# Attention in the second block: two heads to a step, in halves of TensorE's array

## What is computed

```python
logit_own = (jnp.einsum('hqd,hkd->hqk', qc, k_own).astype(jnp.float32) * scale
             - slopes[:, None, None] * dist_own)
logit_own = jnp.where(dist_own >= 0, logit_own, NEG_INF)
...
p = jax.nn.softmax(jnp.concatenate([logit_sel, logit_own], axis=-1), axis=-1).astype(v.dtype)
...
return (jnp.einsum('hqnk,hqnkd->hqd', p_sel, v_g)
        + jnp.einsum('hqk,hkd->hqd', p_own, v_own))
```

## Time and profile before

| | us |
|---|---|
| median of 3 runs | 2004.51 |
| lowest, highest | 2000.12, 2005.65 |
| the profiled execution | 2004.92 |
| its span in the trace | 2003.2 |
| TensorE busy | 1860.3 |
| VectorE busy | 1625.4 |
| ScalarE busy | 709.1 |
| GpSimd busy | 1053.3 |

### The profile page before, as it was taken

One profiled execution on the slowest core, in us unless ns is written; L12 is line 12 of the kernel. 1 busy time (PEld: TensorE's weight loads), 2 busy tenths in 40 slices (PEclk: granted clock), 3 DMA queues, 4 the chain that ended last, 5 costly groups with the idle time before them and its releaser, 6 DMA issues.

```text
span 2003.2 us, 27280 instructions
## 1 busy us (share of the span) xinstructions
PE 1860.3 (93%) x9487; PEld 1596.0 (80%) x9487; DVE 1625.4 (81%) x2566; ACT 709.1 (35%) x1097; POOL 1053.3 (53%) x654
## 2 busy tenths in 40 slices
PE   3997779999999999999999999999999989899985
PEld 2775557999999999999888887878886767778764
DVE  6979977978888888888499999999997867656656
ACT  2343133333333444444333333333334233233441
POOL 1332225588878655555577676767665533342001
PEclk8999789999999999999999999999999999999988
DMA  8241342489989788899899999999982222100011
GB/s 341 87 158 64 130 146 81 162 310 311 315 290 317 247 296 312 297 308 313 321 361 358 350 363 344 363 340 365 353 314 81 93 65 64 63 1 1 1 53 53
DMA packets 160805, 440.34 MB, mean 220 GB/s; under 512 B 13648, under 2 KB 63952, under 8 KB 157648
## 3 DMA queue, kind: packets, MB, share of 16 engines
q1 hardware_dynamic: 65296, 254.71, 36.5%
q0 software_dynamic: 36864, 134.23, 17.7%
q10 hardware_dynamic: 58560, 50.34, 7.6%
HBM read 386.80 MB, written 52.43 MB: 219 GB/s over the span
## 4 chain that ended last, share of the span: by engine, by line
PE 70%; DVE 17%; issue 4%; POOL 4%; ACT 2%; DMA 2%; SPq 0%; DVEq 0%; ACTq 0%; POOLq 0%; PEldq 0%
PE PS L908 30%; PE PS L1075 24%; PE PS L1038 4%; PE PS L1101 4%; POOL w_lo L801 3%; DVE arena L1668 2%; DVE arena L1627 2%; DVE arena L1834 1%; PE PS L1247 1%; PE PS L1229 1%; ACT w_hi L1269 1%; PE PS L923 1%; POOL arena L849 1%; PE PS L999 1%; DMA arena<-in_expert_u_rows,arena 1%
## 5 line engine op out<-in xcount | busy, mean ns | idle before, releaser
L801 POOL TENSOR_TENSOR w_lo<-raw,w_hi 128x1024 fp32r<-128x1024 f32 x300 | 725.0, 2417 | 763.1 <-ACT w_hi L1269 761.9
L1269 ACT ACTIVATE w_hi<-raw 128x1024 fp32r<-128x1024 f32 x332 | 351.9, 1060 | 976.4 <-PE PS L908 616.9
L908 PE MATMUL PS<-act_hi,w_hi 128*128 128x384 f32 (+1 forms) x1632 | 603.5, 370 | 42.3 <-DVE act_lo L1640 14.2
L908 PE MATMUL PS<-act_lo,w_hi 128*128 128x384 f32 (+1 forms) x1632 | 588.3, 360 | 0.0
L908 PE MATMUL PS<-act_hi,w_lo 128*128 128x384 f32 (+1 forms) x1632 | 588.1, 360 | 0.0
L908 PEld LDWEIGHTS PS<-act_hi,w_hi 128*128 128x128 f32 x1632 | 312.7, 192 | 96.4 <-issue 25.9
L908 PEld LDWEIGHTS PS<-act_lo,w_hi 128*128 128x128 f32 x1632 | 312.0, 191 | 25.9
L908 PEld LDWEIGHTS PS<-act_hi,w_lo 128*128 128x128 f32 x1632 | 312.9, 192 | 24.6 <-issue 1.4
L1075 PE MATMUL PS<-w_hi,act_hi 128*128 128x512 f32 x768 | 300.8, 392 | 5.2 <-ACT arena L1390 2.6
L1075 PE MATMUL PS<-w_hi,act_lo 128*128 128x512 f32 x768 | 300.0, 391 | 0.0
L1075 PE MATMUL PS<-w_lo,act_hi 128*128 128x512 f32 x768 | 299.6, 390 | 0.0
(11 more groups left out here) (317 smaller groups left out, 2004.2 us busy)
## 6 DMA issues: line engine op xcount, KB each, us to landing
raw<-in_expert_u SPq DMA_DIRECT2D x128, 512.0 KB
raw<-in_expert_v SPq DMA_DIRECT2D x128, 512.0 KB
raw<-in_w_in SPq DMA_DIRECT2D x52, 512.0 KB
arena<-in_w_ada SPq DMA_DIRECT2D x24, 1024.0 KB, 7.1
gel_d<-arena ACTq DMA_DIRECT2D x64, 384.0 KB
gates_d<-arena ACTq DMA_DIRECT2D x12, 2048.0 KB
arena<-gates_d SPq DMA_DIRECT2D x32, 768.0 KB, 7.1
arena<-gel_d SPq DMA_DIRECT2D x32, 768.0 KB
```

Of the source, the lines that this page charges most:

```text
L801: pool.tensor_tensor(w_lo[:, k % SPLIT, :], raw[:, k % RAW, :], w_hi[:, k % SPLIT, :].bitcast(F32), ALU.subtract).then_inc(lo_split, 1)
L908: mm = pe.matmul(PS[:, bank, 0:n_tok], w[:, k % SPLIT, c * P:(c + 1) * P], x[:, c, 0:n_tok], start=(i == 0 and n == 0), stop=(i == KC - 1 ...
L1269: act.activation(w_hi[:, k % SPLIT, :], raw[:, k % RAW, :], ACT.Copy).then_inc(hi_split, 1)
```

## The change

The units are numbered anew: by pair of heads m, then query block qb, then head e, so that units 2j and 2j + 1 are the two heads of a pair on the same queries.

- Logits: at an even slot TensorE issues both units' matmuls behind each other (step `both_logits`), one from rows 0 to 63 into bank 6, one from rows 64 to 127 into bank 1 (`S_BANK`). Odd slots issue none. VectorE and ScalarE still take a unit a slot.
- Value products: at odd slots alone, for both units, with the head alternating inside the loop over key blocks, so that the output goes to partitions 0 to 63 and 64 to 127 by turns. `PT[e]` replaces `PT[n % 2]`, which is the same buffer.
- All pairs of heads now use bank 0 for value products, since bank 1 holds logits; from the second pair on the first of them waits for `om_ready` of the pair before.
- Projections 32 to 39 swap their two banks; 32 now waits for the last read of bank 1.

```diff
-        if i >= 4:
+        if i >= 4 and i % 2:
             steps.append(("pv", i - 4))
         if 3 <= i < MH * TB + 3:
             steps.append(("turn", i - 3))
         if i < MH * TB:
+            if i % 2 == 0:
+                steps.append(("both_logits", i))
             steps.append(("logits", i))
...
-            return n % 4 if n < 12 else n % 2
+            return n % 4 if n < 12 else n % 2 if n < 32 else (n + 1) % 2
...
+        S_BANK = (6, 1)
...
-                    if 32 <= n < 34:
-                        pe.wait_ge(om_ready, 3 + n - 32)
+                    if n == 32:
+                        pe.wait_ge(l_ready, MH * TB)
+                    elif n == 33:
+                        pe.wait_ge(om_ready, 4)
...
-                if kind == "logits":
-                    m, e, qb = n // 8, n // 4 % 2, n % 4
+                if kind == "both_logits":
+                    m, qb = n // 8, n // 2 % 4
                     if n:
                         pe.wait_ge(l_ready, n)
                     else:
                         pe.wait_ge(rms_ready, 20)
                         pe.wait_ge(p_dve, 20)
-                    s64 = slice(64 * e, 64 * e + 64)
-                    pe.matmul(PS[:, 6, 0:(qb + 1) * P], aq[s64, m, qb * P:(qb + 1) * P],
-                              ak[s64, m, 0:(qb + 1) * P], start=True, stop=True).then_inc(s_full, 1)
+                        pe.wait_ge(p_dve, 32)
+                    for e in range(2):
+                        s64 = slice(64 * e, 64 * e + 64)
+                        pe.matmul(PS[:, S_BANK[e], 0:(qb + 1) * P], aq[s64, m, qb * P:(qb + 1) * P],
+                                  ak[s64, m, 0:(qb + 1) * P], start=True, stop=True).then_inc(s_full, 1)
...
-                    if n % 8 == 0 and m >= 2:
-                        pe.wait_ge(om_ready, m - 1)
+                    if n % 8 == 1 and m:
+                        pe.wait_ge(om_ready, m)
                     pe.wait_ge(pt_ready, n + 1)
                     for kb in range(qb + 1):
-                        mm = pe.matmul(PS[64 * e:64 * e + 64, m % 2, qb * P:(qb + 1) * P],
-                                       avt[:, kb, P * m + 64 * e:P * m + 64 * e + 64], PT[n % 2][:, kb * P:(kb + 1) * P],
-                                       start=(kb == 0), stop=(kb == qb))
-                    mm.then_inc(pv_done, 1)
+                        for e in range(2):
+                            mm = pe.matmul(PS[64 * e:64 * e + 64, 0, qb * P:(qb + 1) * P],
+                                           avt[:, kb, P * m + 64 * e:P * m + 64 * e + 64], PT[e][:, kb * P:(kb + 1) * P],
+                                           start=(kb == 0), stop=(kb == qb))
+                    mm.then_inc(pv_done, 2)
```

More of the change, by code:

```diff
@@ L142, in second_block_steps @@
     steps.append(("gturn", 0))
-    while len([st for st in steps if st[0] == "pv"]) < MH * TB:
+    while len([st for st in steps if st[0] == "pv"]) < MH * TB // 2:
         attend()
@@ L1234, in _ @@
                         pe.wait_ge(pt_ready, n)
-                    for kb in range(n % 4 + 1):
+                    for kb in range(n // 2 % 4 + 1):
                         mm = pe.transpose(PS[:, 7, kb * P:(kb + 1) * P], L[:, n % 3, kb * P:(kb + 1) * P], ident[:, :])
@@ L1504, in _ @@
                     if n >= 32:
-                        act.activation(mx[:, n - 32, :], PS[:, n % 2, :], ACT.Copy).then_inc(mx_ready, 1)
+                        act.activation(mx[:, n - 32, :], PS[:, unit_bank(n), :], ACT.Copy).then_inc(mx_ready, 1)
                 if kind == "tanh":
@@ L1583, in _ @@
                     act.wait_ge(nm_ready, n + 1)
-                    w = (n % 4 + 1) * P
+                    w = (n // 2 % 4 + 1) * P
                     act.activation(L[:, n % 3, 0:w], L[:, n % 3, 0:w], ACT.Exp, bias=nmax[:, n:n + 1],
@@ L2265, in _ @@
                 if kind == "logits":
-                    m, e, qb = n // 8, n // 4 % 2, n % 4
+                    m, qb, e = n // 8, n // 2 % 4, n % 2
                     w = (qb + 1) * P
@@ L2289, in _ @@
                         dve.wait_ge(alo_ready, 32 + m)
-                    v.scalar_tensor_tensor(out=tmp[:, m % 2, :], in0=PS[:, m % 2, :], scalar=0.5, in1=az[:, m, :],
+                    v.scalar_tensor_tensor(out=tmp[:, m % 2, :], in0=PS[:, 0, :], scalar=0.5, in1=az[:, m, :],
                                            op0=ALU.mult, op1=ALU.mult).then_inc(tmp_ready, 1)
```

6 lines of the change are left out of this document (3 added, 3 removed).

## The result

| | before | changed |
|---|---|---|
| median of 4 runs each, us | 2003.2 | 1984.41 |
| lowest, highest | 2000.12, 2005.65 | 1983.03, 1987.07 |
| ratio, with its 95% interval | | 0.9906 [0.9893, 0.9918] |
| span of the profiled execution | 2003.2 | 1981.3 |

The changed kernel is faster by 18.8 us, 0.9%. It is within 1.2 us of the rival "both heads fully side by side", which had 12%. That closeness is in part luck: the rival's mechanism is what happened, but its sum is near because terms that were off by up to 3.3 us cancel (at the end of "Why the forecast was off").

What follows compares the result with a forecast made beforehand. TensorE's time was taken as the kernel's time, busy 82.95 of 83.00 us beside the delta rule. Terms 7.5 + 8.9 - 1.1 - 0.3 - 0.35 - 1.0 + 0.3 = 13.95 us off 2004.9 gave 1991 us; range 1985.0 to 2002.5.

Steps and rivals of the forecast that it cites:

- both heads fully side by side: Rival: all passes of both heads overlap in logits and value products, 14.5 us of overlap, 1985.6 us in all; chance 0.12.
- Two halves of the array at once: Logits and value pairs up to scan 2: in-order overlap of two heads' passes saves 8.9 us, between 0 and 14.5.
- The floor of weight loads: Logits pairs with one key block: four loads of 128 columns fill the pair, cutting its saving from 3.9 to 3.5 us.
- Fewer changes of shape: TensorE's slots up to scan 2: fewer switches between logits, value products and transposes save 7.5 us, whatever the halves do.
- the levels: Stretch from the first logits to scan 2's end, forecast to shrink from 138.4 us by about 15.
- that case: Rival of no overlap: one tile waits for the other, shape savings 7.5 - 0.8 up to scan 2; 2001.3 us, chance 0.15.
- What is given back: Savings of TensorE lost where other engines set the time: 1.1 and 0.3 us up to scan 2, more ahead of scan 3.
- Place (a): 1855.88 to 1866.85 us, where VectorE and ScalarE set the end: TensorE's savings there are mostly lost, -1.1 us.
- The second chain: Chain of other engines ending at 1878.94 us, with slot 22 in it, which gets shorter for nothing: -0.3 us.
- The wider scaling ahead of scan 3: Between scan 2 and scan 3: VectorE's logits 30 grow to 512 columns, its scaling of unit 29 to 384: -0.35 us.
- Scan 3 at half clock: TensorE idles about 3.5 us ahead of scan 3, whose eight matmuls may run at half clock: 0 to 1.9, taken as -1.0 us.
- The tail: After 1928.97 us, units one by one at half clock: 7.4 us with overlap against 7.71 before, +0.3; without overlap -2.2.

## Why the forecast was off

**The step that failed** is the one under "Two halves of the array at once": "If the passes are started in order [...] the second pass of one head can run beside the first pass of the other, while the two passes of one matmul stay behind one another. Then 2m passes of alternating matmuls take m + 1 pass times." The rows of before showed no two tiles of one shape in a row, and the text chose the middle of a range from 0 to 14.5 us "because of the two-pass form". The two-pass form does not matter: both tiles take the same pass at the same time, and 2m passes take m. The term was 8.9; by starts the overlap was 14.4 us (7.7 and 6.7), the upper bound of 14.5, and TensorE's busy time fell by 13.6 of it (7.6 and 6.0). The floor of weight loads was wrong too. It charged 0.4 us for four loads of 128 columns one after another in a pair with k = 1. Such a pair took 0.42 us, as one matmul did (0.41), and in the pair with k = 4 shown above the loads start at 1820.612, .618, .720 and .727, in pairs as well.

**The rule on weight loads.** In this case the two heads of a value product share all rows and differ in columns only, and loads and passes of both ran side by side (1.03 us for sixteen passes, 1.89 in one half). The Trainium skill, TensorE: Matmul & The Clock Gate, Part 3, says that a load overlaps running matmuls only if its row group differs. The measurement differs and decides: the column halves overlapped as fully as the row halves. Even within one half a load ran beside a matmul: in the logits pair the loads at 1820.720 and .727 belong to the second passes, which start at 1821.147 and .153, so each started while its own half's first pass (from 1820.613 and .620) was running. The same part's price for a packed group, one matmul's duration plus some 4 ns a tile, is borne out, with 7 ns here.

**Fewer changes of shape**: right in kind, too small by 1.5 us. 7.5 us was the sum; TensorE's time fell by 9.0 in the run with pairs and no overlap, 6.5 of them in the levels (6.7 was the forecast of that case). The constants from the earlier trace rows hold, and so does the one that no row showed: one transpose ahead of head groups takes 0.16 us (1809.44 to 1809.60), 0.11 of it the pass, so 0.05 was right. Two things are not in the sum. The stretch has two passes of value products and two transposes fewer than before (124 for 126, and 64 for 66), which is 0.4 us. And two transposes ahead of logits take 0.31 us (1820.30 to 1820.61), where they took 0.37 in the earlier trace rows; at 15 such places that is up to 0.9 us, an estimate. Why they became cheaper is open.

**What is given back**: right in kind, far too small, and it is one of the forecast's own signs of being wrong: VectorE's and ScalarE's steps ended TensorE's waits inside the levels. The levels lost 5.3 us to new idle time, where the forecast charged 1.4, and 2.0 with full overlap. Place (a) came out at its price: idle 1.4 before, 2.6 after, 1.2 more for 1.1 forecast. The second chain was put at 0.3 and cost 0.95. The other 3 us are at four places that the forecast did not name, 1869.27 and 1878.44 above all. It had looked for chains in the trace of before where they already ended TensorE's waits, and taken VectorE's share of 70% for room. What it should have done is to follow the pattern of `tokens` to all four chunks: in the kernel before ScalarE's copy of the transposes (line 1592) stood behind the same scaling (1544) at the third chunk, just hidden by TensorE's own work (in order of time, start us, us, instruction):

```profile
1884.95 1.14 ACT L1544 ACTIVATE arena<-PS,small 128x128 f32<-128x128 f32 x4 [2.43 <-DVEq L2220]
...
1886.35 0.28 ACT L1592 ACTIVATE arena<-PS 128x128 f32<-128x128 f32 x1 [0.27 <-ACT arena L1544]
```

Against full overlap, the levels were to be 22.0 - 2.0 = 20.0 us shorter and became 17.3 shorter.

**The wider scaling ahead of scan 3**: -0.35 forecast, -0.54 measured. From ScalarE's squares to scan 3 the chain grew from 7.79 to 8.12 us, the 0.35 to within rounding. The other 0.2 lie ahead of the squares (0.93 and 1.13 us behind the first matmul that follows scan 2), where ScalarE now finishes an exponential before it copies scan 2's result. **Scan 3 at half clock**: -1.0 forecast, -1.5 measured. The mechanism is shown: TensorE idled 3.77 us ahead of it, it ran at 0.50, and 6.51 us came back as soon as TensorE was kept busy, in both runs of the changed kernel kept busy.

**The tail**: +0.3 forecast, +2.7 measured, and it is the same mechanism with its sign turned. The forecast computed the tail at half clock as in the earlier trace rows. Now the idle time and the clock's fall come earlier, at scan 3, and the clock is back when the tail runs. That it is the clock and not the pairs is shown by the two kernels kept busy: 4.87 us for the old tail at full clock and 4.58 for the new one, a gain of 0.3 from pairs. That this is also the forecast's figure is luck, since the forecast worked it out at half clock and with m + 1 passes. So the 1.0 of the forecast for the clock ahead of the tail had a return of 2.4 that it did not look for.

In sum, against the 13.95 us of the forecast: overlap +4.7 (13.6 for 8.9), shapes +1.5, idle time in the levels -3.9, scan 3 and the scaling ahead of it -0.7, the tail +2.4, the stretches that the forecast had no term for +0.5 (2.97 to 2.73, 44.34 to 43.77, 22.18 to 22.47). That is +4.5 and 18.45 us, the table's sum, and would give 1986.5 us from the profiled 2004.9. The medians are 2 us lower still, of which 1.7 is that the profiled execution of before was that much above the median of all four.

The rival with full overlap had 19.35 us in place of 18.45. Its gain from the overlap was 0.9 too high, its gain from shapes 1.5 too low, its loss in the levels 3.3 too low, its loss at scan 3 and the chain ahead of it 0.7 too low, its gain in the tail 2.0 too low, and a gain of 0.5 had no term. A mechanism that is right does not make such a sum right; the agreement to 1 us is in part chance.

**What stays open**: whether TensorE's looking ahead is a limit of three passes or of something else that comes to three here, since only one shape was tried. Why the clock falls inside the levels in some executions and not in others was not tried either. The same code did both, and three kernels (logits with a wait, the same with value products by head, and all logits in one half) had two falls in their one profile. What the traces do show is where: each of the eight falls begins 0.4 to 2.3 us behind the start of an instruction for which TensorE had been idle, either the last of the first place (1847.34 in the changed kernel) or a piece of about 1.4 us for ScalarE's copy at the third chunk. The other two executions of the changed kernel had the same idle pieces and no fall. So the idle time that the change brought stands ahead of the falls, and the forecast, which names a fall inside the levels as a sign against it, had no term for it.

## What to carry to other kernels

Price the overlap of two float32 tiles of one shape at everything: in this kernel a pair of 64-row or of 64-column tiles cost what one costs, over 2 to 8 passes each. Then follow every chain of the other engines through the shortened stretch, hidden ones too, since here a quarter of TensorE's gain became waits for VectorE and ScalarE. Issue such matmuls next to each other with no wait between them, and group by shape, which was worth 6.5 us here beside 10.8 for the overlap. Idle time of TensorE that moved ahead of scan 3 took the clock there (1.5 us) and gave it back in the tail (2.4 us), so cost each stretch behind the change at both clocks.

## What the runs showed of the hardware

- The two passes of a float32 matmul run beside those of another tile in lockstep, 7 ns apart; 16 passes take 1.03 us in two column halves and 1.89 in one, 4 passes of 512 columns 1.06 in two row halves and 1.91 in one.
- With the two heads one behind the other instead of alternating, the second one's first pass starts with the first one's fifth of eight (k = 4), third of six (k = 3) or first of four (k = 2), as the records are read: a pass of a free tile is taken ahead of up to three waiting passes of another.
- A wait for a semaphore between two matmuls cost 0.32 us more than doing them in a row (2.23 and 1.91 us with k = 4, 0.96 and 0.64 with k = 1).
- The granted clock fell to half inside the levels in one of three profiled executions of the changed kernel and in one of two of the one kept busy; such a stretch cost 1.3 us, and all eight falls seen inside the levels began behind idle time of TensorE.
- In the kernel before with five added matmuls the clock fell to half in the middle of three of them, 1.65 us after an idle piece of 1.37 us had ended, and their six passes took 4.4 us.
